# First-layer opening of a two-layer decoder trunk: the scale sums of the first modulation in four 32-column groups of the array, and another order of the first transfers

## The reference, cut to what matters

```python
for l in range(2):
    mod = silu(c) @ w_ada[l] + b_ada[l]
    sh1, sc1, gt1, sh2, sc2, gt2 = split(mod, 6)      # 1024 columns each
    h = rmsnorm(x, g_pre_mix[l]) * (1 + sc1) + sh1
    proj = h @ w_in[l]
    ...                                               # two attentions, gates
    x = x + gt1 * rmsnorm(mixed @ w_out[l], g_post_mix[l])
    h = rmsnorm(x, g_pre_ffn[l]) * (1 + sc2) + sh2
    x = x + gt2 * rmsnorm((silu(h @ w_gate[l]) * (h @ w_up[l])) @ w_down[l], g_post_ffn[l])
```

## Time and profile before

| | |
|---|---|
| Three runs | 866.22 us median (865.53 to 867.44) |
| Profiled execution | span 864.5 us, first to last instruction; its page gives no other time of its own |
| Median less span | 1.7 us |
| TensorE busy | 851.9 us, 99% of the span |
| VectorE, ScalarE, GpSimdE busy | 663.1, 433.2, 103.8 us |
| Read from HBM | 192.29 MB, 224 GB/s over the span |

### The profile page before, as it was taken

The page is one execution under the profiler, slowest core; times in us unless marked ns, Lnnn a source line. Parts: engine busy times, 40 slices in busy tenths (PEclk is TensorE's granted clock), DMA queues, the critical chain, the costliest instruction groups (busy, mean ns, idle before and its releaser), DMA issues.

```text
span 864.5 us, 11670 instructions
## 1 busy us (share of the span) xinstructions
PE 851.9 (99%) x4226; PEld 708.9 (82%) x4226; DVE 663.1 (77%) x1172; ACT 433.2 (50%) x676; POOL 103.8 (12%) x79
## 2 busy tenths in 40 slices
PE   9999999999999999999999999999999999999997
PEld 8987888888878887878888778888888788888885
DVE  4787999898886778697489799988788855645843
ACT  4465545565656533434366544465565634434522
POOL 1610110301201012030310030030030000000300
PEclk9999999999999999999999999999999999999999
DMA  8986665757426688777536766566744364674511
GB/s 346 362 341 225 238 219 200 273 204 297 151 94 244 228 301 304 286 271 279 193 147 230 265 224 255 193 234 234 264 147 171 124 266 174 246 251 181 203 66 49
DMA packets 34363, 194.10 MB, mean 225 GB/s; under 512 B 4481, under 2 KB 4481, under 8 KB 16770
## 3 DMA queue, kind: packets, MB, share of 16 engines
q1 hardware_dynamic: 32978, 189.64, 59.7%
q0 software_dynamic: 1328, 3.71, 1.4%
HBM read 192.29 MB, written 1.05 MB: 224 GB/s over the span
## 4 chain that ended last, share of the span: by engine, by line
PE 91%; DVE 3%; DMA 2%; issue 1%; ACT 1%; SPq 0%; DVEq 0%; ACTq 0%
PE ps L1285 26%; PE ps L1287 25%; PE ps L1286 25%; PE ps L1363 4%; DMA wide_t<-ada_first 2%; PE ps L1418 2%; PE ps L1455 1%; PE ps L1307 1%; PE ps L1446 1%; PE ps L1308 1%; PE ps L1440 1%; PE ps L1439 1%; PE ps L1438 1%; PE ps L1372 1%; PE ps L1417 1%
## 5 line engine op out<-in xcount | busy, mean ns | idle before, releaser
L839 DVE TENSOR_TENSOR w_lo<-raw,w_hi 128x2048 fp32r<-128x2048 f32 (+1 forms) x132 | 308.1, 2340 | 50.1 <-ACT w_hi L570 48.5
L1285 PE MATMUL ps<-w_hi,t_hi 128*128 128x512 f32 (+2 forms) x784 | 307.6, 392 | 0.0
L1287 PE MATMUL ps<-w_hi,t_lo 128*128 128x512 f32 (+2 forms) x784 | 301.2, 384 | 0.0
L1286 PE MATMUL ps<-w_lo,t_hi 128*128 128x512 f32 (+2 forms) x784 | 300.6, 383 | 0.0
L570 ACT ACTIVATE w_hi<-raw 128x2048 fp32r<-128x2048 f32 (+1 forms) x132 | 249.9, 1895 | 17.5 <-DMA raw<-w_stream 9.5
L1285 PEld LDWEIGHTS ps<-w_hi,t_hi 128*128 128x128 f32 x784 | 147.3, 188 | 29.8 <-issue 1.3
L1287 PEld LDWEIGHTS ps<-w_hi,t_lo 128*128 128x128 f32 x784 | 147.2, 188 | 29.6
L1286 PEld LDWEIGHTS ps<-w_lo,t_hi 128*128 128x128 f32 x784 | 147.5, 188 | 27.4
L484 POOL PARTITION_ALL_REDUCE wide_t<-wide_t x10 | 64.2, 6421 | 586.4 <-DVE wide_t L857 586.4
L857 DVE SCALAR_TENSOR_TENSOR wide_t<-ada,cs,wide_t 128x1024 f32<-128x1024 f32 x80 | 106.5, 1331 | 0.3
L1285 PE MATMUL ps<-w_hi,m_hi 128*128 128x512 f32 x240 | 99.5, 415 | 0.3
(11 more groups left out here) (179 smaller groups left out, 848.5 us busy)
## 6 DMA issues: line engine op xcount, KB each, us to landing
raw<-w_stream SPq DMA_DIRECT2D x128, 1024.0 KB, 5.8
ada<-w_ada SPq DMA_DIRECT2D x80, 512.0 KB, 4.5
wide_t<-ada_first SPq DMA_DIRECT2D x5, 1024.0 KB, 9.6
wide_t<-gains POOLq DMA_DIRECT2D x7, 512.0 KB, 5.7
mixed<-ada_first SPq DMA_DIRECT2D x3, 1024.0 KB, 6.4
raw<-w_stream SPq DMA_DIRECT2D x4, 656.0 KB, 6.6
x<-x_in SPq DMA_DIRECT2D x1, 1024.0 KB, 5.0
out<-x SPq DMA_DIRECT2D x4, 256.0 KB, 2.0
```

The source lines that it names most:

```text
L839: nc.vector.tensor_tensor(w_lo[:, U % RING, 0:n], raw[:, U % RAW, 0:n], w_hi[:, U % RING, 0:n].bitcast(F32), ALU.subtract).then_inc(s_lo, 1)
L1285: nc.tensor.matmul(dst, hi, w_h, start=first, stop=False)
L1286: nc.tensor.matmul(dst, hi, w_l, start=False, stop=False)
L1287: return nc.tensor.matmul(dst, lo, w_h, start=False, stop=last)
```

## The change

- The stream of blocks is divided. Scale weights come as four transfers of 1 MiB (`scale_first`, one for a pair of blocks, two buffers), shift weights as eight of 512 KiB (`shift_first`, four buffers, two of them those of `ada`).
- The scale sums of a pair are made by `partial_rows(p)`: eight float32 matmuls with silu(c) stationary, repeated in 32 columns, and 256 columns of weights moving. Matmul k writes partitions 32 (k mod 4) and up, so four groups hold partial sums. ACT copies them (`copy_rows`), and `scale_columns(p)` adds them with one matmul per block against the column `pick` (ones in rows 0, 32, 64 and 96), which also turns them from a row into a column; the transposes follow as before.
- x is first in SyncE's queue; the small inputs are issued by ACT.
- The order of transfers: units 3 and 4 come last. Unit 5 waits for all eight shift sums as well.
- On ACT and DVE the work goes by pairs, and the splits stand elsewhere.
- The fills are 4, 4 and 24 in place of 4, 14, 2, 4 and 4.

```diff
-FIRST_RING = 3
-FIRST_ORDER = ((0, False), (0, True), (1, False), (2, False), (1, True), (3, False), (2, True), (4, False),
...
+FIRST_ORDER = (("scale", 0), ("unit", 0), ("shift", 0), ("shift", 1), ("unit", 1),
+               ("scale", 1), ("shift", 2), ("shift", 3), ("unit", 2),
+               ("scale", 2), ("shift", 4), ("shift", 5), ("scale", 3), ("shift", 6), ("shift", 7),
+               ("unit", 3), ("unit", 4))
...
-FIRST_SPLIT = (0, 2, 3, 6)
-FIRST_FILL = (4, 14, 2, 4, 4)
+FIRST_FILL = (4, 4, 24)
...
+            sp.wait_ge(s_first_sh, KT)
             for l in range(DEPTH):
...
+            def copy_rows(p):
+
+                act.wait_ge(s_rows, p + 1)
+                nc.scalar.activation(scale_rows[p % 2], ps[:, QKT + 2 * p % 4, 2 * P:4 * P], ACT.Copy).then_inc(s_rows_sb, 1)
...
+            for p in range(PAIRS):
+                copy_rows(p)
+                if p == 0:
+                    split_hi(0, 0)
+                first_hi(2 * p)
+                first_hi(2 * p + 1)
+                if p < 2:
+                    split_hi(0, p + 1)
+            split_hi(0, 3)
+            act.wait_ge(s_ang, 1)
+            nc.scalar.activation(ang[:, 4:6], ang[:, 2:4], ACT.Sin).then_inc(s_sin, 1)
+            split_hi(0, 4)
...
+            split_lo(0, 0)
+            for p in range(PAIRS):
+                first_sums(2 * p)
+                first_columns(2 * p)
+                first_sums(2 * p + 1)
+                first_lo(2 * p)
+                first_columns(2 * p + 1)
+                first_lo(2 * p + 1)
+                if p < 2:
+                    split_lo(0, p + 1)
+            split_lo(0, 3)
+            split_lo(0, 4)
...
+            def partial_rows(p):
+
+                bank = QKT + 2 * p % 4
+                pe.wait_ge(s_scale_in[p % 2], 16 * (p // 2 + 1))
+                if p > 1:
+                    pe.wait_ge(s_first_h, 2 * p - 3)
+                for k in range(KT):
+                    j = 32 * (k % 4)
+                    ins = nc.tensor.matmul(ps[j:j + 32, bank, 2 * P:4 * P], cs_wide[:, k, :],
+                                           scale_at[p % 2][:, k * 2 * P:(k + 1) * 2 * P], start=k < 4, stop=k > 3)
+                ins.then_inc(s_rows, 1)
+
+            def scale_columns(p):
+
+                pe.wait_ge(s_rows_sb, p + 1)
+                for i in range(2):
+                    if p > 1:
+                        pe.wait_ge(s_first_h, 2 * p + i - 3)
+                    k = 2 * p + i
+                    nc.tensor.matmul(ps[:, QKT + k % 4, 2 * P:3 * P], scale_rows[p % 2][:, i * P:(i + 1) * P],
+                                     pick[:, :].broadcast_to([P, P]), start=True, stop=True)
+                    turn(ps[:, QKT + k % 4, :], [hbuf[:, t, k * P:(k + 1) * P] for t in range(TT)], s_mod)
...
+                partial_rows(0)
                 pe.wait_ge(s_const, 32)
...
+                scale_columns(0)
+                fill(2, ones[:, :], ones[:, :], P, FIRST_FILL[2])
+                for k in range(2):
+                    first_products(k, (0,))
+                partial_rows(1)
                 for k in range(2):
                     first_products(k, (1,))
+                scale_columns(1)
                 first_products(2, (0, 1))
...
+                first_products(3, (0, 1))
+                for p in range(2, PAIRS):
+                    partial_rows(p)
+                    scale_columns(p)
+                    first_products(2 * p, (0, 1))
+                    first_products(2 * p + 1, (0, 1))
```

More of the change, by code:

```diff
@@ L256, in hybrid_decoder_trunk @@
         s_cols = sem("columns_landed")
-        s_first = [sem(f"first_block_landed{i}") for i in range(FIRST_RING)]
+        s_scale_in = [sem(f"first_scale_block_landed{i}") for i in range(2)]
+        s_shift_in = [sem(f"first_shift_block_landed{i}") for i in range(4)]
         s_gain = sem("gain_landed")
@@ L1174, in _ @@
             nc.vector.memset(ones[:, :], 1.0).then_inc(s_ones, 1)
+            link(nc.vector.memset(pick[:, :], 0.0))
+            for j in range(4):
+                ins = nc.vector.memset(pick[32 * j:32 * j + 1, :], 1.0)
+            ins.then_inc(s_pick, 1)
             dve.wait_ge(s_ones, 1)
@@ L1185, in _ @@
             dve.wait_ge(s_c_rows, 1)
-            for k in range(KT):
-                first_sums(k)
-                if k:
-                    first_lo(k - 1)
-                first_columns(k)
-                if k in FIRST_SPLIT[:-1]:
-                    split_lo(0, FIRST_SPLIT.index(k))
-            split_lo(0, RING - 2)
-            first_lo(KT - 1)
-            split_lo(0, RING - 1)
+            split_lo(0, 0)
[10 more added lines that the diff above has]
+            split_lo(0, 4)
             for l in range(DEPTH):
```

103 lines of the change are left out of this document (41 added, 62 removed).

## The result

| | before | after |
|---|---|---|
| Median of four runs each, same chip | 866.01 us (865.53 to 867.44) | 873.28 us (873.12 to 873.55) |
| Ratio to before, 95% interval | | 1.0077 [1.0064, 1.0090] |
| Span of the profiled execution | 864.5 us | 871.3 us (+6.8) |
| Chunk 2 starts | 45.16 us | 50.95 us (+5.79) |
| Index transposes behind it start | 50.64 us | 57.65 us (+7.01) |

What follows compares the result with a forecast made beforehand. TensorE bounds the kernel, so only the opening up to chunk 2 counts. The chain through three engines moves chunk 2 from 45.16 to 49.3, +4.1 us: span 868.6, plus 1.7 for the median gives 870.4 us; range 868.0 to 874.4.

Steps and rivals of the forecast that it cites:

- 10 us of TensorE work disappear, but the staggering does too: Opening, summary of the chain: TensorE's saving is outweighed by lost overlap between blocks; chunk 2 shifts by +4.1 us.
- 15.1 - 4.3 - 1.8: TensorE in the opening: 15.1 us of blocks removed; partial rows at 1.07 per pair and scale columns at 0.22 per block added.
- two-group matmuls of the earlier trace: Matmuls in two groups of 64 partitions at 57.29 us: 0.86 passes for 1.28 of streaming; basis of 1.07 per pair.
- 874.0 rival: Partial rows on TensorE: groups do not overlap fully, 1.9 us per pair, 3.6 in all, 874.0 us; chance 0.10.
- The small inputs move to ACT's queue: hidden: Start of ACT: five issues and the table load cost nothing, since ACT waits 3.84 us for x; at most about 2 uncovered.
- the arrival of the first scale weights at 9.3: Start of the chain: first scale weights land at 9.3 us, then the first pair's partial rows run, done at 11.4.
- the sine: ACT's tail behind unit 3's split, ahead of unit 4: counted as 0.2 us.
- the second rival: TensorE's clock in the opening: fills stay slow or waits lower it, 1 to 3.5 us more, 871.5 to 874; chance 0.15.
- Faster because transfers set the pace: Opening: unit 3's transfer sets the start, chunk 2 at 41.7, -3.5 us, 862.7 us; chance 0.07.
- once the chain reaches the high part of block 7 by 37.5: Condition for transfers to set chunk 2's start: block 7's high part at 37.5 instead of 44.6, 7 us sooner.

Runs made afterwards that it cites:

- e4: The changed kernel with the partial rows made by the whole array, one group of 128 columns, instead of four groups: 882.52 us, 1.0183 to before.
- e9: The refitted stagger with small inputs on SyncE and 14 fills, but row sums made by the whole array: 873.13 us, 1.0081 to before.
- e5: The changed kernel with small inputs on SyncE, orders of TensorE, ACT and DVE refitted to a stagger, 14 fills for 24: 864.09 us, 0.9974 to before.
- e1: The changed kernel with the five small inputs issued by SyncE again, around x: 871.99 us, 1.0069 to before.
- e8: The kernel before with only x put first on SyncE and the five small inputs issued by ACT: 869.80 us, 1.0037 to before.
- e2: The changed kernel with the splits of unit 3 and the sine put ahead of pair 3: 870.65 us, 1.0049 to before.
- e6: The changed kernel with 7 more fills in TensorE's wait behind the scale columns of pair 3: 873.48 us, 1.0079 to before.
- e10: The refitted stagger with 14 fills, but small inputs on ACT's queue as in the change: 869.04 us, 1.0032 to before.
- e11: The refitted stagger with small inputs on ACT's queue and the sine back between units 3 and 4: 868.89 us, 1.0027 to before.

## Why the prediction was right, and what it mis-sized

**Right: the direction, its chain and its main price.** Each step against the row:

| step | forecast | row of after |
|---|---|---|
| partial rows, pairs 1 to 3 | 1.07 us | 1.07 us |
| first partial rows | 9.3 | 11.51 |
| low part of unit 1 done | 23.3 | 25.06 |
| pair 2 (rows to rows) | 8.0 | 7.99 |
| rows of pair 3 | 38.9 | 41.09 |
| high part of block 7 done | 44.6 | 46.57 |
| chunk 2 | 49.3 | 50.95 |

From the second row on the chain runs parallel to the forecast, 1.65 to 2.2 us late. "10 us of TensorE work disappear, but the staggering does too" is what e4, e9 and e5 show from both sides: the groups are worth 9 us, and with them the order and the place of the small inputs decide between 873.3 and 864.1. (The forecast's own terms give 15.1 - 4.3 - 1.8 = 9.1 us and not 10; the chain did not use that number.) That price came from the two-group matmuls of the earlier trace rows. The Trainium skill (TensorE: Matmul & The Clock Gate, Part 3) says that matmuls of packed tiles start and end in program order without overtaking; it was the rule behind the 874.0 rival, and the 1.07 us here speaks against full waiting between groups, since 1.9 would then have been the duration. The total came near 874 all the same, by other terms.

**Step that failed first: "The small inputs move to ACT's queue: hidden".** I argued that ACT waits for x anyway, and counted only ACT's time for the issues. That is hidden. Not hidden is that the transfers land late, 7.5 to 11.9 us after their issue: `cs` is made at 8.81 us, the squares of x and the row of silu(c) follow it on ACT, and TensorE starts when that row is done, at 11.41. e1 puts the cost at 1.3 us; the same edit costs 3.3 in e8. The term that the chain had in this place, the arrival of the first scale weights at 9.3, was not the one that decided: in the change they are there at 8.3, a microsecond sooner than forecast. In e1, where they are issued 2.4 us later, they land at 10.1 and do decide.

**Step that is missing: the sine.** The forecast counted it as 0.2 us in ACT's tail and did not follow who waits for it. Moved behind unit 3, it hands GpSimd its tables at the very time of DVE's longest operations, and the index transposes wait 0.97 us. About 0.6 us of DVE's delay is the meeting with GpSimd's clearing at 53.95. e2 removes the wait. So the account is: 5.79 at chunk 2, of which 4.1 was forecast and 1.65 is what is left there of the late start (e1 takes back 1.48); 0.97 at the index transposes; 0.25 between them, since chunk 2's first matmul takes 0.12 us longer out of a wait and its last one runs out before the next wait. That is 7.01 at the index transposes, and the span grew by 6.8.

**Rivals.** The clock: it did fall (46 to 49 us, to 0.50 at the lowest), as the second rival says, but e6 shows that it cost nothing here, because ACT was last to arrive. The three executions at a mean clock of 0.999, no shorter than the profiled one, say the same. Faster because transfers set the pace: false for the change (DMA share 0.35 from 36 us), and e5 shows what it takes; chunk 2 came at 42.71 there against the 41.7 that I gave for this case. The condition in it, "once the chain reaches the high part of block 7 by 37.5", is nearly what e5 reaches (38.4).

**Left open.** Why small transfers on a second queue land so late was not taken apart; e1, e8 and e10 change queue and place together. In every kernel GpSimd stands for 8 to 11 us between the positions and its first angles (10.3 before, 10.7 in e10) without a releaser that the profile shows; this is more than the positions were late, and nothing here explains it. Why the granted clock falls behind the wait of pair 3 in some executions and not in others stays open. e5 still has 1.38 us in which TensorE waits for ACT's copies of chunk 0 behind unit 4's split; another order there was not tried.

## What to carry to other kernels

When an edit removes work from the fullest engine, look at what it does to the stagger: sum the chain through all engines for one period, old and new, before believing in the saving. Here the same saving of 9 us gave +0.77% in one order and -0.26% in another; the better order needs its inputs in time, too, for with the small inputs on ACT's queue it is at +0.32% (e10). Follow every moved operation to its reader, however small it is: late small inputs, of which GpSimd got the 1 KB of positions last, lengthened the span of e10 by 3.7 us, and a late sine of 0.24 us, with what it ran into, cost the changed kernel 0.97 us.

## What the runs showed of the hardware that I had not expected

- **Small transfers on a second queue.** Beside large transfers of SyncE's, 4 KB on ACT's queue, issued at 1.3 us, land after 7.5 us, and 1 KB, issued at 2.2, after 11.2 us; on SyncE's queue ahead of all weights `cT` takes 1.7 and the positions, behind x, 5.0.
- **GpSimd beside DVE.** Operations of 32 columns take 0.25 to 0.30 us alone and 2.10 (e11) or 2.46 (before, at 22.08) beside a two-input DVE operation of 128 x 2048, and end 0.11 us (42.78 and 42.67) and 0.15 us behind it. The Trainium skill (SBUF — State Buffer, SBUF: two separate sides) says that the two engines share one pair of ports, taken as a lock for a whole instruction, so that the loser is blocked rather than slowed. The trace agrees: the copies at 48.57, 4.40 us for two, last as long as the two splits beside them (4.50 us). The other way round, beside GpSimd's clearing of 0.95 us at 53.95, DVE operations of 0.17 and 0.22 us take 0.88 and 0.86.
- **The clock.** In the profiled execution of the change the granted clock fell behind the wait that ends at 45.40 (0.50 from 46 to 49 us), but not behind the equal waits at 29.49 and 37.46, and not at all in e2 with the same waits. What a fall costs depends on who is last: nothing in the change (e6), 2.4 us in e11.
- **Four groups fully side by side.** 16 float32 entries of 256 columns in four 32-column groups take 1.07 us, against 3.62 for the whole array: 3.4 times.
